# Two chunks of the output projection: half of their sum over k as seven half-size products

## What is computed

```python
m = jax.nn.sigmoid(ma) * ya + jax.nn.sigmoid(mb) * yb
return jnp.einsum('bsd,de->bse', m, w_out)      # 256 x 2048 times 2048 x 2048
...
x = x + hybrid_mixer(...)
return rmsnorm(x, g_final)
```

## Time and profile before

| | us |
|---|---|
| median of 3 runs | 739.93 (739.87 to 740.32) |
| the profiled execution, its own time | 740.02 |
| its span in the trace | 738.2 |
| PE busy in the span | 728.4 |
| DVE busy | 560.0 |
| ACT busy | 438.3 |
| POOL busy | 84.2 |

### The profile page before, as it was taken

One profiled execution on the slowest core, in us unless ns is written; L12 is line 12 of the kernel. 1 busy time (PEld: TensorE's weight loads), 2 busy tenths in 40 slices (PEclk: granted clock), 3 DMA queues, 4 the chain that ended last, 5 costly groups with the idle time before them and its releaser, 6 DMA issues.

```text
span 738.2 us, 9729 instructions
## 1 busy us (share of the span) xinstructions
PE 728.4 (99%) x3538; PEld 609.4 (83%) x3538; DVE 560.0 (76%) x724; ACT 438.3 (59%) x652; POOL 84.2 (11%) x105
## 2 busy tenths in 40 slices
PE   8999999999999999999999999999999999999996
PEld 6998888888888888888888888888888888888886
DVE  6775798779669778877978976988998657655552
ACT  7963667466656565666656667667567544444531
POOL 0000223103010201010302010202020000001110
PEclk9999999999999999999999999999999999999999
DMA  8668465776956676785586766566677656756632
GB/s 330 212 209 332 146 228 203 250 225 236 340 171 237 220 248 224 271 289 192 203 273 199 270 247 262 198 259 224 221 249 248 200 193 228 292 191 187 193 140 115
DMA packets 47230, 168.97 MB, mean 229 GB/s; under 512 B 5256, under 2 KB 5264, under 8 KB 46672
## 3 DMA queue, kind: packets, MB, share of 16 engines
q1 hardware_dynamic: 46064, 164.97, 64.6%
q10 hardware_dynamic: 864, 1.84, 0.7%
q0 software_dynamic: 256, 1.54, 0.5%
HBM read 166.23 MB, written 2.11 MB: 228 GB/s over the span
## 4 chain that ended last, share of the span: by engine, by line
PE 94%; DVE 2%; issue 2%; DMA 1%; ACT 1%; SPq 0%; DVEq 0%; POOLq 0%; POOL 0%; ACTq 0%
PE Z L342 29%; PE Z L343 28%; PE Z L344 28%; PE Z L503 3%; PE A L444 1%; DVE w_lo L845 1%; PE A L410 1%; DMA w_raw<-in_w_main 1%; PE B L426 1%; PE Dk L435 1%; PE B L423 1%; DVE gates L912 1%; PE C L453 0%; ACT w_hi L614 0%; PE A L461 0%
## 5 line engine op out<-in xcount | busy, mean ns | idle before, releaser
L845 DVE TENSOR_TENSOR w_lo<-w_raw,w_hi 128x1024 fp32r<-128x1024 f32 (+1 forms) x240 | 290.5, 1215 | 113.4 <-ACT w_hi L614 110.9
L614 ACT ACTIVATE w_hi<-w_raw 128x1024 fp32r<-128x1024 f32 (+1 forms) x235 | 243.7, 1044 | 184.5 <-PE Z L344 162.3
L342 PE MATMUL Z<-w_hi,hT_hi 128*128 128x512 f32 (+2 forms) x720 | 274.4, 381 | 0.5 <-DVE w_lo L845 0.5
L344 PE MATMUL Z<-w_hi,hT_lo 128*128 128x512 f32 (+2 forms) x720 | 272.7, 379 | 0.0
L343 PE MATMUL Z<-w_lo,hT_hi 128*128 128x512 f32 (+2 forms) x720 | 272.7, 379 | 0.0
L342 PEld LDWEIGHTS Z<-w_hi,hT_hi 128*128 128x128 f32 x720 | 135.3, 188 | 26.9 <-issue 0.6
L344 PEld LDWEIGHTS Z<-w_hi,hT_lo 128*128 128x128 f32 x720 | 135.3, 188 | 25.4
L343 PEld LDWEIGHTS Z<-w_lo,hT_hi 128*128 128x128 f32 x720 | 135.3, 188 | 24.5
L342 PE MATMUL Z<-w_hi,sum_hi 128*128 128x512 f32 x256 | 101.2, 395 | 0.0
L344 PE MATMUL Z<-w_hi,sum_lo 128*128 128x512 f32 x256 | 99.8, 390 | 0.0
L343 PE MATMUL Z<-w_lo,sum_hi 128*128 128x512 f32 x256 | 99.7, 390 | 0.0
(11 more groups left out here) (184 smaller groups left out, 567.4 us busy)
## 6 DMA issues: line engine op xcount, KB each, us to landing
w_raw<-in_w_main SPq DMA_DIRECT2D x283, 512.0 KB, 4.1
x_and_g<-in_w_main SPq DMA_DIRECT2D x16, 512.0 KB, 7.1
w_raw<-in_w_fl SPq DMA_DIRECT2D x8, 264.0 KB, 3.0
o_T<-in_x SPq DMA_DIRECT2D x1, 2048.0 KB, 7.9
x_and_g<-in_xT SPq DMA_DIRECT2D x4, 256.0 KB, 5.9
gates<-c_rows_dram POOLq DMA_DIRECT2D x1, 1024.0 KB, 6.1
z_sb<-in_g_final SPq DMA_DIRECT2D x1, 1024.0 KB, 9.9
x_and_g<-in_xT ACTq DMA_DIRECT2D x3, 256.0 KB, 7.3
```

Source lines behind the costliest of these rows:

```text
L342: pe.matmul(acc, a_hi, b_hi, start=first, stop=False)
L344: return pe.matmul(acc, a_lo, b_hi, start=False, stop=last)
L614: act.activation(w_hi[:, t % RING, 0:cols_of(t)], weights(t), ACT.Copy).then_inc(hi_ready, 1)
L845: dve.tensor_tensor(w_lo[:, t % RING, 0:n], weights(t), w_hi[:, t % RING, 0:n].bitcast(fp32), ALU.subtract).then_inc(lo_ready, 1)
```

## The change

The output stage is now 30 jobs before `LAST` in place of 24. Chunk 2 comes first, as 8 plain tiles. Chunks 0 and 1 keep plain tiles only for the second half of k (4 tiles each). The first half of k of both chunks together (two token blocks, two column chunks, two k halves) is made of seven forms of two sum tiles each, spread between the plain tiles. Counted from 0, the jobs are: plain 0 to 3 (chunk 2); P1 in 4, 5; then pairs of a plain tile and a sum tile: 6 to 9 with P5 in 7, 9; 10 to 13 with P6 in 11, 13; 14 to 17 (chunk 0 begins) with P7 in 15, 17; 18 to 21 with P4 in 19, 21; then plain 22 (chunk 1), P2 in 23, 24, plain 25, P3 in 26, 27, plain 28, 29.

Prices in other places: ACT also writes m unsplit (`m32`) for the first two merged chunks; POOL makes the four sums of token blocks (`m_sum`); ACT and DVE split them (`msum_hi`, `msum_lo`); POOL adds x to four blocks that are on their way (`near_residual`); the squares of chunks 0 and 1 stand behind the last four copies of `LAST`. P4, P2 and P3 are accumulated directly on chunk 0's and chunk 1's banks.

```diff
+LAST_JOB = OUT_JOB + 30
+JOBS = LAST_JOB + TILES
+OUT_PLAIN = [(2, j) for j in range(TILES)] + [(0, j) for j in range(4, TILES)] + [(1, j) for j in range(4, TILES)]
+SUMS_BEHIND = [0, 0, 0, 2, 1, 1, 1, 1, 1, 1, 1, 1, 2, 2, 0, 0]
...
+OUT_FORMS = (P1, P5, P6, P7, P4, P2, P3)
+OUT_TARGET = {P4: (1, 0), P2: (0, 0), P3: (0, 1)}
...
 # SP, load(job)
                     if f == P1:
...
+                        elif g == GROUPS:
+                            sp.wait_ge(msums_ready, 4)
...
 # DVE, fold(g, f)
+                if g == GROUPS:
+                    if f == P6:
+                        dve.wait_ge(kept, 2 * g + 2)
+                        dve.tensor_tensor(out_21, acc, out_11, ALU.add).then_inc(folded, 1)
+                        dve.wait_ge(folded, 5 * g + 1)
+                        dve.tensor_tensor(out_22, out_21, out_12, ALU.add).then_inc(folded, 1)
+                    if f == P7:
+                        dve.wait_ge(near_ready, 2)
+                        dve.tensor_tensor(out_22, acc, out_22, ALU.add).then_inc(folded, 1)
+                        dve.tensor_tensor(out_21, acc, out_21, ALU.add).then_inc(folded, 1)
+                    return
...
 # DVE, the output stage
+            for job in range(OUT_JOB, LAST_JOB):
+                if form_ended(job) is not None and form_ended(job)[1] not in (P1, P5):
+                    fold(*form_ended(job))
+                if job + 5 in SUM_OF and sum_parts(SUM_OF[job + 5])[1] in (P5, P6, P7, P4):
+                    add(SUM_OF[job + 5])
+                if job < OUT_JOB + 2:
+                    msum_lo_part(job - OUT_JOB)
+                if job == OUT_JOB + 2:
+                    merged_lo(3)
+                if OUT_JOB + 3 <= job < OUT_JOB + 5:
+                    msum_lo_part(job - OUT_JOB - 1)
+                t = job + RING
+                if t < LAST_JOB:
+                    split(t)
+                else:
...
+                if job in OUT_OF and OUT_OF[job] in ((2, TILES - 1), (1, 5), (1, TILES - 1)):
+                    residuals({(2, TILES - 1): 2, (1, 5): 0, (1, TILES - 1): 1}[OUT_OF[job]])
...
 # ACT, merged_hi(n) and the output stage
+                if n < 2:
+                    for b in range(2):
+                        act.activation(m32[:, 4 * n + 2 * b:4 * n + 2 * b + 2, :], (A, B)[b][:].rearrange("p (a n) -> p a n", a=2),
+                                       ACT.Copy, scale=0.5).then_inc(m32_ready, 1)
...
+                if job in OUT_OF and OUT_OF[job] == (0, 5):
+                    squares(2)
             for j in range(4, TILES):
...
+            squares(0)
+            squares(1)
...
 # POOL
+                a, b, op = ((m32[:, m_near, tok1], m32[:, m_far, tok1], ALU.add),
+                            (msums_raw[0], m32[:, m_near, tok0], ALU.subtract),
+                            (m32[:, m_far, tok0], msums_raw[1], ALU.subtract),
+                            (m32[:, m_near, tok0], m32[:, m_near, tok1], ALU.subtract))[i]
...
+            def near_residual(m, n):
+                sl = slice(n * CHUNK, (n + 1) * CHUNK)
+                y_block = y_sb[:, m, sl] if (m, n) != (0, 1) else y_sb[:, 1, CHUNK:2 * CHUNK]
+                pool.tensor_tensor(y_sb[:, m, sl], y_block, x_res[:, m, sl], ALU.add).then_inc(near_ready, 1)
...
+            pool.wait_ge(folded, 5 * GROUPS + 1)
+            near_residual(0, 0)
+            pool.wait_ge(folded, 5 * GROUPS + 2)
+            near_residual(0, 1)
+            pool.wait_ge(folded, 5 * GROUPS + 4)
+            near_residual(1, 0)
+            near_residual(1, 1)
```

More of the change, by code:

```diff
@@ L264, in weights, with blocks_of, form_bank @@
         def weights(job):
-            return chain[:, SUM_OF[job] % QUARTERS, :] if in_chain(job) else raw_slot(job)
+            return chain[:, sum_parts(SUM_OF[job])[2], :] if in_chain(job) else raw_slot(job)
+        def blocks_of(g):
+            if g < GROUPS:
+                return [gates[:, g, m, branch, :] for m in range(M_TILES) for branch in range(2)]
+            return [y_sb[:, m, branch * CHUNK:(branch + 1) * CHUNK] for m in range(M_TILES) for branch in range(2)]
+        def form_bank(g, f):
+            if g < GROUPS:
+                return Z[2 + (FORMS * g + f) % 2]
+            if f in OUT_TARGET:
+                m, n = OUT_TARGET[f]
+                return Z[2 * (1 - OUT_PLACE[n] % 2) + m]
+            return {P1: C, P5: Dk, P6: C, P7: Dk}[f]
         def k_view(buf, t, k, n):
@@ L344, in split_product, with tile @@
                 return pe.matmul(acc, a_lo, b_hi, start=False, stop=last)
-            def tile(t, pair, stat_hi, stat_lo, k0, ks, n, first, last):
+            def tile(t, pair, stat_hi, stat_lo, k0, ks, n, first, last, closed=True):
                 pe.wait_ge(hi_ready, t + 1)
@@ L353, in tile @@
                         mm = split_product(Z[2 * pair + m][:, 0:n], stat_hi[:, k0 + kk, tok], stat_lo[:, k0 + kk, tok],
[L354 removed]
+                                           hi[:, kk], lo[:, kk], first and kk == 0,
+                                           last and closed and kk == ks - 1)
                 mm.then_inc(w_used, 1)
@@ L575, in _ @@
                         merged_transposes(n - 1)
[L576 to L579, removed]
+            for job in range(OUT_JOB, LAST_JOB):
+                if job in OUT_OF:
+                    n, j = OUT_OF[job]
+                    first = 0 if n == 2 else 4
+                    if j == first:
+                        banks_free(25 + OUT_PLACE[n])
+                    if n == 2:
                         pe.wait_ge(mT_lo_ready, j + 1)
-                    tile(OUT_JOB + 8 * n + j, 1 - n % 2, hT_hi, hT_lo, 2 * j, 2, CHUNK, j == 0, j == TILES - 1)
-                    if n == 0 and j == 1:
+                    tile(job, 1 - OUT_PLACE[n] % 2, hT_hi, hT_lo, 2 * j, 2, CHUNK, j == first,
+                         j == TILES - 1, closed=n != 0)
+                    if job == OUT_JOB + 1:
                         merged_transposes(3)
+                else:
+                    sum_tile(SUM_OF[job])
             banks_free(28)
@@ L763, in _ @@
                     evacuate(HEAD_OF[job][0])
-                if job in SUM_OF and SUM_OF[job] % QUARTERS == QUARTERS - 1:
-                    g, f, _ = sum_parts(SUM_OF[job])
-                    if f in (P1, P5):
-                        keep(g, f)
+                if form_ended(job) is not None and form_ended(job)[1] in (P1, P5):
+                    keep(*form_ended(job))
                 split(job + RING)
@@ L1089, in _ @@
                     fox_gate(FOX_OF[job][0])
-                if job in SUM_OF and SUM_OF[job] % QUARTERS == QUARTERS - 1 and sum_parts(SUM_OF[job])[1] not in (P1, P5):
-                    fold(*sum_parts(SUM_OF[job])[0:2])
+                if form_ended(job) is not None and form_ended(job)[1] not in (P1, P5):
+                    fold(*form_ended(job))
                 if job + 5 in SUM_OF and sum_parts(SUM_OF[job + 5])[1] in (P5, P6, P7, P4):
```

163 lines of the change are left out of this document (111 added, 52 removed).

## The result

| | us |
|---|---|
| kernel before, median of 12 runs | 739.89 (739.72 to 741.39) |
| changed kernel, median of 12 runs | 741.57 (741.14 to 743.92) |
| ratio after / before | 1.0024 [1.0017, 1.0031] |
| predicted | 737.3, range 736.8 to 739.6 |
| profiled execution of the changed kernel, own time; span | 742.35; 740.5 |

A forecast was written before the change was run, and what follows sets the result against it. The prediction took PE to be the bound, busy 728.4 of 738.2 us. From 740.0 it subtracted PE's gain of 2.7 and took every other cost as 0, giving 737.3, range 736.8 to 739.6.

The forecast's parts named there:

- PE's gain: Output stage on PE: 14 sum tiles replace 8 plain tiles, 84 matmuls instead of 96, saving 2.72 us.
- Rival 4: Sum tiles on PE cost more than 0.227 per matmul, for instance 0.25, adding 1.9 us; result 739.2, chance 0.06.
- SP's wait for the token sums: P1's loads, and all loads queued behind, wait for POOL's four token sums; taken to cost 0.
- ACT's additions: Extra copies, msum_hi and keep on ACT fit its 1.65 us of waiting per tile; costed at nothing.
- The DVE's chain to job 18 without POOL: From job 12's end the DVE needs 8.4 us, PE 9.4, so job 18 is ready 1.0 us early.
- POOL beside the DVE: POOL's additions and multiplications near job 18 slow each DVE instruction by 0.3 us; taken as 0, bounded by 1.5.
- The term of 0.9 - 1.0: At job 18, POOL's two additions cost the DVE 0.9 us against a cushion of 1.0, leaving 0.1.
- Rival 2: POOL and DVE take turns in whole instructions; PE waits 1.5 us at job 18; result 738.9, chance 0.08.
- Rival 1: The DVE is late at job 18 or 21 by 0.5 to 1.4 us; result 738.2, chance 0.22.
- Rival 3: Loads become the bound from job 22 on, at landings above 5.0 us; result 741.9 at 6.0, chance 0.09.
- The moved squares: Squares of chunks 0 and 1 behind LAST's copies, and chunk 2's behind job 20's copy, cost 0.
- The tail: Behind PE's last work the instructions are the same as before, so it costs 0.

The follow-up runs named there:

- The repaired kernel: The changed kernel with additions of x on the DVE, POOL's multiplications after the last split and its token sums held until merged chunk 2 is written; 737.42, again 737.74 us.
- e7: e6 with POOL's four token sums also waiting until merged chunk 2 is written; 737.42 us, ratio 0.9965 to the kernel before.
- e12: e7 run a second time, unchanged; 737.74 us, ratio 0.9967 to the kernel before.
- m1_turns: Separate kernel: eight DVE additions alone (9.17 us) and beside POOL additions of 128 to 1024 columns (10.98 to 13.46) or memsets; one phase has a PSUM operand.
- e4_near_memset: Changed kernel with POOL's four additions of x replaced by memsets of 384 columns, so the output lacks x in two column chunks; 739.00 us, ratio 0.9989.
- e8: Changed kernel with only POOL's six multiplications by g_final moved behind the DVE's last split, additions of x still on POOL; 739.99 us, ratio 1.0000.
- e5: Changed kernel without the four additions of x, and with POOL's multiplications by g_final waiting for the DVE's last split; 738.54 us, ratio 0.9979.
- e6: Changed kernel, full computation, with the four additions of x on the DVE and POOL's multiplications behind the DVE's last split; 738.14 us, ratio 0.9968.
- e10: e7 with the squares of chunks 0 and 1 put back behind their residuals, where they stood before the change; 739.05 us, ratio 0.9984.
- e1: Changed kernel without POOL's four additions of x and the waits for them, so the output lacks x in two column chunks; 739.80 us, ratio 0.9989.

## Why the prediction was wrong

- **PE's gain: right.** 12 matmuls fewer and a sum tile still 1.36 (677.22 to 678.58). The repaired kernel ends at 737.4 and 737.7, 0.1 and 0.4 from the 737.3 of the sum, and its PE is busy 725.4 where 725.7 was forecast.
- **Rival 4, dearer sum tiles: refuted** by the same.
- **SP's wait for the token sums, 0: right.** The four sums on POOL ended at 633.7, inside the 631.6 to 641.7 that were set out. P1's loads were issued from 635.16, right behind the late split, and PE lost nothing in jobs 0 to 17.
- **ACT's additions, 0: right.** With POOL out of the way, the same additions cost PE nothing (e7).
- **The DVE's chain to job 18 without POOL, 1.0 us early: right.** In e12 the split of job 18 ends at 678.90 + 1.22 = 680.12 and PE takes the job at 681.18, 1.06 behind it.
- **POOL beside the DVE: the failed step.** The prediction took +0.3 per DVE instruction, "by the nearer row, rows 8". The instructions that POOL did there were of 128 and 256 columns, of 0.4 to 0.6 us each alone, and the row that had grown by 0.4 (1.63) stood behind the one of 256. So +0.2 to +0.4 was not a rate but one whole POOL instruction in front of each DVE instruction, and it has to be scaled with POOL's width: 1.1 for 512 columns, as 2.32 and 2.31 in place of 1.22 show. The term of 0.9 - 1.0 (nothing late) should have been 2 x 1.1 - 1.0 = 1.2, and with the 0.15 from the end of the split (683.92) to the matmul (684.07), which the sum left out, 1.35; 1.41 was lost. The same rate let the prediction put the POOL instructions behind job 18 at nothing, and its token sums weren't weighed against the DVE at all; they cost the further 1.0, 0.8 and 0.35. That the two rows agree with the theory of turns just as well as with a rate was not seen; that POOL's own instructions took "three times as long" in the earlier trace rows (1.4 per instruction, one DVE instruction each) should have pointed to it.

The Trainium skill (SBUF — State Buffer, "Who interferes with whom") has the rule that was weighed against this row: a DVE instruction with two inputs in SBUF and a GpSimd instruction that reads SBUF exclude each other, while a DVE instruction with at most one SBUF input, outside the modes that use both ports, or a GpSimd instruction that only writes, does not disturb. The traces agree: m1_turns shows the first with 1.07 us per POOL instruction of 512 columns, one SBUF input beside a PSUM operand and memsets with none, and e4_near_memset the memset inside the kernel. The rule was right against my reading of the rows. One row of e12, at the end of this document, has one SBUF input and was held up all the same; no run here tells in which mode it ran.

- **Rival 2, turns in whole instructions: the right mechanism with too low a price, and a chance of 0.08.** It was worked out at job 18 alone (1.5, measured 1.41), and what follows was said to be "mostly covered by the delay PE already has". It wasn't: PE's delay of 1.4 is used up by the four POOL instructions from 688.74 on (7 splits, 12.48 us in place of 7 x 1.13 = 7.9: 4.6 more, 1.1 per POOL instruction), and PE lost 1.0 at 696.64 and 698.86 and 0.8 to 0.9 in `LAST`, besides 0.35 at the merge, where the prediction had looked at POOL's token sums only as something SP waits for. e8 and e5 show both parts separately. Had every instruction of POOL in the stage been priced, the rival would have stood on the slower side.
- **Rival 1** (late at job 18) saw the place, for another reason. e5, e6 and e12, with the same DVE list up to job 18 and nothing on POOL, lose nothing there, so the DVE's load by itself doesn't make it late.
- **Rival 3, the loads: a consequence, not the cause.** Its signature was there, ACT waiting for DMA and PE for ACT. But landings were 4.4, under the 5.0 from which it was to start, and the lost time went away in e5 when POOL fell silent. The loads were issued late, not slow. ACT's waits for DMA in `LAST` remain in e5 and e12 and cost PE nothing.
- **The moved squares, 0: right in what it costs, wrong in what it is worth.** e10 puts 1.3 to 1.6 us on it, which the prediction did not see.
- **The tail: right.** From the first residual of the last part to the end of the span it is 740.5 - 721.90 = 18.6, before 738.2 - 719.55 = 18.65.

What stays open: the share of the median's +1.68 that lies outside the 1.3 accounted for, and why the 12 and 11 runs of e1 and e4 scatter over 2.6 and 2.8 us, where the five of e7 stay within 0.4 and the five of e12 within 0.8.

## What to carry to other kernels

Price a POOL instruction that reads SBUF, beside a DVE that reads two SBUF operands, as a whole turn taken from the DVE, by POOL's own width (here 1.1 us for 512 columns, half for 256, double for 1024), and do this for every POOL instruction in the stretch where the DVE has no idle time, not only at the narrowest place. When a row of a shared stretch shows a mild growth, divide it by the size of the neighbour's instructions before using it as a rate. Work that isn't urgent (here the multiplications by g_final) is better behind the last instruction of the contended stretch, and work can be cheaper on a full DVE than on a POOL that is free but takes turns with it.

## What the hardware showed that I had not expected

Work on the engine with the least to do was dearer than on the one with the most: with the four additions on POOL and the six multiplications early the kernel is 3.4 us slower (4.1 by the ratios) than with the additions on the DVE itself, 0.68 each, and the multiplications late, where PE then loses nothing to them. Even a DVE instruction of two columns was held up: this one of e12, 0.17 in the changed kernel, stood beside POOL's multiplications and ended at 716.93, just behind the one that POOL had begun at 715.62 and ended at 716.91.

```profile
715.78 1.15 DVE L1281 TENSOR_SCALAR y_part<-ms 128x2 f32<-128x2 f32 x1
```

It reads one SBUF operand only. m1_turns had nothing of this form, so why it waited is not shown.
